# ScalarE, not SyncE, starts twenty of the weight loads of a hybrid decoder layer

## What is computed

```python
proj = rms_norm(x, norm1_g) @ w_in                     # 2048 -> 512 + 3*512 + 3*1024 + 8
y_pool, y_conv = pool mixer, short convolution         # of the first 2048 columns
k_past = cache_k[l, page_table].reshape(db, past, N_HEADS, HEAD_DIM)   # 8 sequences x 32 pages of 128 rows
v_past = cache_v[l, page_table].reshape(db, past, N_HEADS, HEAD_DIM)
y_att = softmax(q @ [k_past, k] + forget bias) @ [v_past, v]           # sample; the prompt attends to itself
x = x + concat(rms_norm(y_pool), rms_norm(y_conv), rms_norm(y_att)) @ w_o
x = x + (silu(dwconv(xn2 @ w_up[a]) + b) * (xn2 @ w_up[gate])) @ w_down
```

## Time and profile before

| | us |
|---|---|
| median of three runs | 2793.99 |
| range of the runs | 2789.83 to 2795.3 |
| the profiled execution | 2790.12 |
| its span, first to last instruction | 2788.5 |

### The profile page before, as it was taken

One profiled execution on the slowest core, in us unless ns is written; L12 is line 12 of the kernel. 1 busy time (PEld: TensorE's weight loads), 2 busy tenths in 40 slices (PEclk: granted clock), 3 DMA queues, 4 the chain that ended last, 5 costly groups with the idle time before them and its releaser, 6 DMA issues.

```text
span 2788.5 us, 50733 instructions
## 1 busy us (share of the span) xinstructions
PE 2604.3 (93%) x19733; PEld 2336.0 (84%) x19733; DVE 1419.9 (51%) x5626; ACT 729.8 (26%) x1019; POOL 161.1 (6%) x326
## 2 busy tenths in 40 slices
PE   6688789999888799889999999999999999999998
PEld 4686677777675355569999999999999999999998
DVE  5698867877867612244434343434343434343433
ACT  4222123333332311132222222222222222222221
POOL 0100111111111122100000000000000000000000
PEclk8888889999999899989999999999999999999999
DMA  9678999999999887652222222222222222222221
GB/s 306 242 248 308 334 328 370 361 363 361 338 337 367 328 292 260 211 187 91 92 91 92 91 91 92 91 91 91 91 91 91 91 91 91 91 91 91 92 91 65
DMA packets 272292, 524.55 MB, mean 188 GB/s; under 512 B 16148, under 2 KB 181693, under 8 KB 270740
## 3 DMA queue, kind: packets, MB, share of 16 engines
q1 hardware_dynamic: 218717, 365.71, 37.8%
q0 software_dynamic: 39760, 142.46, 13.8%
q10 hardware_dynamic: 13575, 13.14, 1.4%
HBM read 501.84 MB, written 17.76 MB: 186 GB/s over the span
## 4 chain that ended last, share of the span: by engine, by line
PE 72%; DVE 11%; DMA 11%; issue 3%; SPq 2%; ACT 1%; POOL 0%; DVEq 0%; POOLq 0%; ACTq 0%
PE ps L752 71%; DMA t_r<-in_cache_k 9%; DVE t_r L1862 7%; DMA t_r<-in_cache_v 1%; SPq L633 1%; PE ps L755 1%; DMA t_wraw<-in_w_in 1%; SPq L637 0%; DVE t_stg L1748 0%; DVE t_wlr L1687 0%; DVE t_auxL L1687 0%; DVE t_work L1687 0%; DVE t_S L1862 0%; DVE t_xl L1687 0%; SPq L686 0%
## 5 line engine op out<-in xcount | busy, mean ns | idle before, releaser
L752 PE MATMUL ps<-t_xh,t_wh 128*128 128x260 f32 (+1 forms) x4352 | 1079.1, 299 | 39.2 <-DVE t_wlr L1687 23.6
L752 PE MATMUL ps<-t_xl,t_wh 128*128 128x260 f32 (+1 forms) x4352 | 1052.2, 293 | 0.0
L752 PEld LDWEIGHTS ps<-t_xh,t_wh 128*128 128x128 f32 x4352 | 744.1, 193 | 169.4 <-issue 115.1
L1687 DVE TENSOR_TENSOR t_wl<-t_wraw,t_wh 128x1024 fp32r<-128x1024 f32 x296 | 362.4, 1225 | 842.9 <-ACT t_wh L1275 842.9
L1275 ACT ACTIVATE t_wh<-t_wraw 128x1024 fp32r<-128x1024 f32 x376 | 398.5, 1060 | 1481.9 <-PE ps L752 1367.6
L752 PEld LDWEIGHTS ps<-t_xl,t_wh 128*128 128x128 f32 x4352 | 743.2, 193 | 10.7 <-issue 1.4
L752 PE MATMUL ps<-t_xh,t_wl 128*128 128x260 f32 (+1 forms) x3072 | 676.9, 294 | 0.0
L1862 DVE CUSTOM_DVE_ANT_0 t_r<-t_r,t_work 128x128 f32<-128x128 f32 x2048 | 456.1, 290 | 174.9 <-DMA t_r<-in_cache_k 158.9
L752 PEld LDWEIGHTS ps<-t_xh,t_wl 128*128 128x128 f32 x3072 | 487.6, 189 | 11.8
L752 PE MATMUL ps<-t_xh,t_wlr 128*128 128x260 f32 x1280 | 374.7, 293 | 0.0
L752 PE MATMUL ps<-t_hh,t_wh 128*128 128x260 f32 x1408 | 282.4, 282 | 3.4 <-issue 3.4
(11 more groups left out here) (312 smaller groups left out, 1228.2 us busy)
## 6 DMA issues: line engine op xcount, KB each, us to landing
t_r<-in_cache_k SPq DMA_DIRECT2D x256, 512.0 KB, 6.6
t_r<-in_cache_v POOLq DMA_DIRECT2D x256, 512.0 KB, 7.0
t_wraw<-in_w_up SPq DMA_DIRECT2D x44, 2048.0 KB, 7.9
t_wraw<-in_w_down SPq DMA_DIRECT2D x22, 2048.0 KB, 7.8
t_wraw<-in_w_in SPq DMA_DIRECT2D x21, 2048.0 KB, 15.5
t_wraw<-in_w_o SPq DMA_DIRECT2D x11, 2048.0 KB, 13.7
scr_x<-t_r POOLq DMA_DIRECT2D x1, 4160.0 KB, 14.6
t_work<-in_x_prompt SPq DMA_DIRECT2D x4, 1024.0 KB, 6.7
```

Source lines behind the costliest of these rows:

```text
L752: return pe.matmul(out, lhsT, rhs, start=start, stop=stop)
L1687: return dve.tensor_tensor(out, in0, in1, op)
```

## The change

The twenty loads of raw pairs of slots 3 to 79 leave SP's program, with their wait for `w_used`. ACT issues them, behind `keep_half(s // 2, 1)` of the same slots, which has already waited for the same value of `w_used`, and ahead of `head(0, s + 4)`. Slots of the buffer, sources, sizes and semaphores are the same. The raw pairs of later slots stay with SP.

```diff
@@ SP's slots
                 for n, g in zip(kp, kg):
                     page(kring, k_pages, k_loaded, k_used, g, *divmod(n, PAGES))
-                if s % 4 == 3 and s < CHUNKS:
-                    n = (s - 3) // 4 + 2
-                    sp.wait_ge(w_used, 4 + 4 * (n - 1))
-                    source, col = (w_in_v, TILES[2 * n] * P) if n < R_O else (w_o_v, OUT_ORDER[2 * (n - R_O)] * P)
-                    sp.dma_start(wraw[:, n % 2, :].rearrange("p (k n) -> p k n", k=KT),
-                                 source[:, :, col:col + 2 * P]).then_inc(w_loaded[n % 2], 16)
@@ ACT's slots
                 if s < CHUNKS and s % 2:
                     head(0, s + 3)
                     keep_half(s // 2, 1)
+                    if s % 4 == 3:
+                        n = (s - 3) // 4 + 2
+                        source, col = (w_in_v, TILES[2 * n] * P) if n < R_O else (w_o_v, OUT_ORDER[2 * (n - R_O)] * P)
+                        act.dma_start(wraw[:, n % 2, :].rearrange("p (k n) -> p k n", k=KT),
+                                      source[:, :, col:col + 2 * P]).then_inc(w_loaded[n % 2], 16)
                     head(0, s + 4)
```

## The result

The changed kernel takes 2854.2 us (median; 2847.8 to 2854.9), the kernel before 2794.6 us beside it. The ratio is 1.0214, its interval 1.0198 to 1.0230: 59.5 us slower, where 27 us faster was forecast. The profiled execution is the fastest of the four, 2847.8 us, with a span of 2846.2.

The account below looks back on a forecast made before the run. It took DVE, late for keys behind raw pairs in SP's queue, to bound 84 to 260 us, and PE 400 to 700. Gains of 35 less 1, 3 and 4 made 27 us: 2767 us, range 2753 to 2786, chance 0.55.

Parts of the forecast that it names:

- Moved past ACT's queue: ACT's stores and `load_y` now stand behind 2 MB: 1 us for held issues, 3 us for the raw pair's landing.
- gains of the later stages: Less waiting on late keys: 10 us from 260 to 400, 3 from 400 to 700, 9 from 700 to 885.
- gains on the key side: Key pages no longer behind raw pairs in SP's queue: DVE's waits for them fall from 149 us to under 50.
- first stage: From 84 to 260 us, DVE the bound: its key waits come off the time, 13 us taken, 15.5 at most.
- Added to ACT: 20 issues of 0.43 us, 9 us on ACT, costed at nothing while ACT has slack.
- First price: ACT held issuing a store behind the pair, 7.8 us against 6.4 idle: 1 us, bounds 0 and 62.
- Second price: Pair lands at 21 us beside keys and values; PE notices at about 29 us: 3 us, ends 0 and 40.
- second rival: ACT held in a store's issue or waiting for the pair beyond PE's need: 2811 us, 2800 to 2830; chance 0.14.
- Slot 79: ACT's pair followed at once by `load_y`, 4 MB in another order, ACT perhaps held: 4 us, bounds -2 and 12.
- bandwidth rival: Bandwidth binds, DVE's wait moves from key page to raw pair: 2794 us, 2789 to 2799; chance 0.18.

## Why the prediction was wrong

**The step that failed** is *Moved past ACT's queue*. It set 1 us for holds and 3 us for the landing against a gain of 35; undoing the two by halves gives back 59 us. The gains of the later stages, 22 of the 35 us, didn't come either.

**The gains on the key side came as forecast.** DVE's waits for keys were to fall from 149 us to under 50; they fell to 36, no issue of SP is held, and the first stage was to gain 13 us and gained 11.5. It is DVE that bound there, and with the pair issued elsewhere the gain reached the end (12 us in the kernel that stops at slot 19).

**The gains of later stages, 10 + 3 + 9, did not.** The wait for keys went, and with it PE's waits on `t_wlr` after 260, but waits for ACT took their place. In no kernel here do slots 20 to 79 get more than about 3 us shorter (623 us with the halves on SP, 626 before, one execution each).

**Added to ACT: 20 issues.** Right: 0.39 us each, in slack; issued within 1 us of the copy to `t_projS`.

**First price, the holds.** It was costed at 1 us. Three things in it were wrong:

- The size of a hold. It was taken from SP's, 7.8 us; the longest on SP was 9.0. That was a key page's place behind a pair, with no keys beside the pair. On ACT the pair has two other queues beside it, and five of the fourteen holds are 12 to 17 us. With the keys kept behind the pair the longest is 8.1, so it is the keys beside it that make them long.
- The slack. 6.4 us was read off one slot. The table above gives it four times, as hold less pause: 5.8, 5.3, 1.2 and 4.9 us. The 49 us of holds in these four cost PE 32.
- What stands behind the store. The prediction named the accumulator that PE needs two slots later. In two of the four it was the next prompt head's logarithm, which PE's transposes need within 8.5 us (433.3 to 441.8), in the others the copies and exponentials right behind the store (`copy` to `t_work`, L1476). The step was to list what is queued behind the waiting instruction, and it listed the store's own next reader.

The upper bound, 62 us, was written down, and the sum took 1 us of it.

**Second price, the landing: mis-sized, and its deadline wrong.** The forecast was 21 us, the measured median 24.1, the longest 37.1. The prediction let about five key pages at most go ahead of the pair; the queues carried eight from 622 to 649, as many as the two and a half slots used that the pair was under way. Worse was the deadline. PE was to notice at 29 us; landing less pause gives 21.1, 19.2 and 24.6 us. The forecast of 21 was thus itself at the edge, and a us beyond it reached PE. For the pair of slot 27 the edge was far lower. 31.6 us less the pause of 20.2 is 11.4, and the kernel before gives nearly the same: 19.1 less 9.3 is 9.8. There ACT has a whole chain of work behind `head` that PE waits for, and the prediction had taken off only two of its steps. This could be read before the change. PE's second wait from 260 to 400 is not in the earlier trace rows:

```profile
PE ps L752 <- issue: 9.3, 1, 9.3
```

It stood behind a pair that was already too late on SP's queue, with ACT waiting 10.8 us for it. The term was 3 us; this price alone was some 32 us by the run with both halves at once, and the second half a slot later gave another 11.

**The form of the rivals.** The second rival, "ACT is held or starved", is what happened, with both of its mechanisms, and at 2854 beyond its range of 2800 to 2830. Its chance of 0.14 rested on "the pages stop by themselves when the pair is late", which there was true only after eight pages. The test given for it, landings over 29 us, would have read the median of 24.1 as a sign against it, though five of the twenty took over 30; the deadline was the error, not the direction.

**Slot 79.** Cost 4 us, measured -1.4: no sign of it. `load_y` is held, 3.6 and 6.5 us, and slot 79 to the end takes 1901.4 us, before 1902.8.

**The bandwidth rival.** It would have left the time where it was. The mean rate fell from 366 to 320 GB/s in the stretch from 400 to 700, so it was not bandwidth that bound the stretch. It did set how late a pair was, as the engines were full while one was under way; between the pairs they were short of work. The Trainium skill says, in "DMA: Bandwidth & Descriptors", section "Issuing engines are not separate DMA queues", that issuing from several engines saves only the time on a sequencer, which is usually small beside the transfer. That rule would have given no change, and the traces disagree: the change costs 2.1%; in slots 3 to 19 the other queue gains 12 us, by order; and an issue is not small where it is held, 14.5 us of ACT for a store of 256 KB. The kernels with the halves a slot apart do end near no change (1.0018 and 1.0003), but as a gain of 13 to 15 us in slots 3 to 19 and a loss of 15 to 20 in slots 32 to 79.

**The two together.** In steps, by ratio: 1.0214 as changed; 1.0099 when the first chunk doesn't wait for the second half; 1.0042 when the stores are off ACT too; 1.0003 when the second half comes a slot later. That is 32 + 16 + 11 = 59 us, and brings the time back to that before. The shares depend on the order: the stores taken off first are worth 4 us by the ratios, with a landing that grows from 24 to 30 us. They have wide intervals, too: the 16 us can be 6 or 25. What stays open is why the halves on ACT end at 2795 and not at the forecast's 2767. ACT waits 195 us for halves there, against 84 with the halves on SP, PE's pause of 20.2 us is still 19.3, against 13.0, and slots 32 to 79 take 506 us instead of 486; that this is the share of the packets again was not separated.

## What to carry to other kernels

A DMA moved to a computing engine takes that engine's later DMAs, and its computing, with it: list everything in that engine's program behind the next issues, and find the reader of each, before a hold is costed at nothing. Before it gets a slower way, look in the old trace for a place where the same load was already late, and read the deadline there; a wait put down to "issue" can be such a place. Before a large load is moved to another queue, split it and let the small urgent ones in between: here that was worth 0.9% on the old queue, and the move cost 2.1%. Where two causes of lateness may hide each other, take each away with the other gone too.

## What the runs showed of the hardware

- An issue on a queue that still holds a pair of 2 MB can be held until the pair has landed in part (the store of 433.3 until 447.8, the pair landing at 454.1), on SP and on ACT alike: up to 9.0 us on SP before, and up to 16.78 us on ACT where three queues share the engines. With the pair in two halves a slot apart it was 26.6 us in 6 issues, with the whole pair 112 us in 14, with the same stores.
- In the earlier trace rows a queue of 1 KB packets got a half to a quarter of the bytes of the others. In 27 us here the pair's queue carried 2.10 MB, key pages 4.19, value pages 3.80. A pair on ACT's queue landed after 24 us (median) with key pages beside it, and after 16.8 without.
- The pair landed 6 us earlier where ACT was held (24.1) than where it wasn't (30), with the same loads. Why was not shown.
- While a pair was under way the 16 DMA engines moved about the same before and after the change (379 and 375 GB/s from 400 to 700). What changed was how long it was under way in that stretch, 125 and 168 us, and the rate in between, 356 and 250 GB/s.
